# A product-key expert kernel: eight second-index rows in one operation, the gate moved into the first index's rows, and those rows dealt to three engines

## The chip, the cores and the metric

The kernel runs on one core of a Trainium2 chip. The metric is the device time of one execution in microseconds. Before the change three executions took 3919.23, 3922.02 and 3924.52 us; the median is 3922.02 us.

## The reference, cut to what matters

One inference step of a hybrid backbone, two layers over 128 context tokens and 512 latent tokens, all in float32. Each layer has a mixing half (pooling, gated linear attention, windowed attention) and a retrieval half; the change lies in the second:

```python
def _peer(h, wq, subkeys, u, v):
    q = (hf @ wq).reshape(n, PEER_HEADS, 2, PEER_QUERY_DIM // 2)
    s = jnp.einsum('nhpd,hpkd->nhpk', q, subkeys).astype(jnp.float32)
    sv, si = lax.top_k(s, PEER_TOPK)
    cand = (sv[:, :, 0, :, None] + sv[:, :, 1, None, :]).reshape(n, PEER_HEADS, PEER_TOPK * PEER_TOPK)
    cand_idx = (si[:, :, 0, :, None] * PEER_N_KEYS + si[:, :, 1, None, :]).reshape(n, PEER_HEADS, PEER_TOPK * PEER_TOPK)
    top_v, top_pos = lax.top_k(cand, PEER_TOPK)
    experts = jnp.take_along_axis(cand_idx, top_pos, axis=-1)
    gates = jax.nn.softmax(top_v, axis=-1).astype(h.dtype)
    ...
        act = jax.nn.gelu(jnp.einsum('td,tkd->tk', xb, u[eb]), approximate=False)
        return jnp.einsum('tk,tkd->td', gb * act, v[eb])
```

So each token picks 128 experts (8 heads, 16 each) out of 128 x 128, each given by a first index i, a second index j and a gate.

## The kernel before, in words

The 640 tokens are five blocks of 128. Blocks 0 and 1 gather the rows of their experts. The other three (`DB`, latent tokens) go the dense way: TensorE multiplies their activations with the whole table (`u_stage`, 128 stages of j), ScalarE applies Gelu, VectorE multiplies with a gate matrix G, and TensorE multiplies with the second table (`v_stage`). G is zero but for the 128 chosen experts of a token.

G is made in the stage that the change touches. For each of the three blocks (k = 1, 2, 3 in the code, blocks 1 to 3 in this text) TensorE turns the indices and gates so that the 128 choices of a token lie along the partitions (`turn`), and ScalarE copies them out (`turned_out`, L1706 to L1714) to `ijgT`: first index, second index, gate. Then each token gets two one-hot matrices of 128 choices by 128 keys: A marks the first index (`agrp`), B the second with the gate as its value (`bring`). TensorE multiplies them (`place`, L1907): one product is the 128 x 128 gate matrix of the token. In the trace each such product is two records, so a group of four tokens is 8 records.

A block is eight steps of 16 tokens; a step is four groups of four tokens, g0 to g3 below. Groups are numbered n over all blocks. Who makes what:

- B: VectorE, 16 operations of 128 columns in a step (`scatter_rows`, L1542), in a ring of 16 tokens.
- A: a ring of four groups (`A_GRP`). ScalarE marks the even n, g0 and g2 (`mark_rows`: four Abs of key minus index, then one Relu of 1 - x over all four tokens, L1726 and L1728). GpSimd marks the odd n, g1 and g3 (L1374).
- ScalarE also takes each group's product out of PSUM (`spread`, L1738), and after the evacuation of group n it marks group n + 4. There are two PSUM banks for the products:

```python
                        if n >= 2:
                            pe.wait_ge(g_out, n - 1)
```

so TensorE starts group n when group n - 2 has been evacuated.

No scheduler stands behind this: every engine's order is written by hand, and semaphores join them. `b_made`, `a_made` and `p_made` count finished one-hots, `g_mm` finished groups, `g_out` evacuated groups, `tr_out` turned indices. VectorE runs the routing of the next token block (top 16, candidates, indices, `route`) between the steps of `scatter_rows`; a new block's `turn` needs that routing's end (`gated`, after ScalarE's Exp in L1698). TensorE fills the time between steps with queries, scores and, in blocks 2 and 3, with `u_stage`. In block 1 ScalarE has other work in between: the square and the root of the fifth row block (L1656, L1661, L1662), copies of queries, turned rows and scores (L1680, L1670, L1674, L1690).

Of the kernel before, what the change touches and what calls it, by code (L numbers as in the profile page):

```python
# [12 lines left out]
ALU = mybir.AluOpType  # L13
# [27 lines left out]
JGRP = 4  # L41
CHUNK = 32
UR, VR, GR = 3, 3, 3
A_GRP, B_TOK = 4, 16
ADA_RING = 5
NMOD = 6 * KT

# [15 lines left out]
def build(nc, a, out, depth=DEPTH):  # L63
    sems = []

    def sem(name):
        s = nc.alloc_semaphore(name)
        sems.append(s)
        return s
# [102 lines left out]
    sc_mm, sc_ready, sc_read = sem("sc_mm"), sem("sc_ready"), sem("sc_read")  # L172
    ex_in, ex_out, ij_ready = sem("ex_in"), sem("ex_out"), sem("ij_ready")
    tr_mm, tr_out, a_made, b_made = sem("tr_mm"), sem("tr_out"), sem("a_made"), sem("b_made")
    p_made = sem("p_made")
    g_mm, g_out, g_sent = sem("g_mm"), sem("g_out"), [sem("g_sent0"), sem("g_sent1")]
    ut_mm, ut_gelu, ut_gated, vt_mm = sem("ut_mm"), sem("ut_gelu"), sem("ut_gated"), sem("vt_mm")
    routed, row_used = sem("routed"), sem("row_used")
# [184 lines left out]
    for l in range(depth):  # L363
# [913 lines left out]
        with nc.Block() as block:  # L1277
# [84 lines left out]
            @block.gpsimd  # L1362
            def _(pool):
                for n in range(ND // 4):
                    if act_marks(n):
                        continue
                    d, q = n // (P // 4), n % (P // 4)
                    if n < A_GRP:
                        pool.wait_ge(x_kept, 16 * len(DB))
                    pool.wait_ge(tr_out, d + 1)  # L1370
                    if n >= A_GRP:
                        pool.wait_ge(g_mm, n - A_GRP + 1)
                    for t in range(4):
                        pool.tensor_scalar(agrp[n % A_GRP][:, t], iota128[:, :], ijgT[:, d % 2, 0, 4 * q + t:4 * q + t + 1], 0.0,  # L1374
                                           ALU.add, ALU.is_equal).then_inc(p_made, 1)
                pool.wait_ge(sc_mm, NB)
                pool.wait_ge(routed, 1)
                for at in range(NROWS):
                    kind, b = ROUNDS[at // SLOTS]
                    q = at % SLOTS  # L1380
                    tab = tab_u if kind == "u" else tab_v
                    if at == EARLY - 2:
                        pool.wait_ge(g_mm, ND // 4)
                    if at == FIRST:
                        pool.wait_ge(routed, 2)
                    if before[at] is not None:
                        pool.wait_ge(row_used, before[at] + 1)
                    pool.indirect_dma_start(ring[slots[at]], None, tab, bass.IndirectOffsetOnAxis(  # L1388
                        ap=eidx[:, b * SLOTS + q:b * SLOTS + q + 1], axis=0)).then_inc(row_landed[slots[at]], 16)

            @block.vector
            def _(dve):
# [141 lines left out]
                def scatter_rows(d, step):  # L1534
                    if step == 0:
                        dve.wait_ge(tr_out, d + 1)
                        dve.wait_ge(x_kept, 16 * len(DB))
                    for t in range(16 * step, 16 * step + 16):
                        n = d * P + t
                        if n >= B_TOK and t % 4 == 0:  # L1540
                            dve.wait_ge(g_mm, (n - B_TOK) // 4 + 1)
                        dve.tensor_scalar(bring[:, n % B_TOK], iota128[:, :], ijgT[:, d % 2, 1, t:t + 1],  # L1542
                                          ijgT[:, d % 2, 2, t:t + 1], ALU.is_equal, ALU.mult).then_inc(b_made, 1)

                residual(0)
                mean(0)
# [103 lines left out]
            def _(act):  # L1650
# [55 lines left out]
                def turned_out(d):  # L1706
                    act.wait_ge(tr_mm, d + 1)
                    if d == 0:
                        act.wait_ge(xn_ready, 4)
                    if d >= 2:  # L1710
                        act.wait_ge(b_made, (d - 1) * P)
                        act.wait_ge(p_made, (d - 1) * (P // 2))
                    c.link(act.activation(ijgT[:, d % 2, 0], ps[:, 0, 0:P], ACT.Copy, scale=-1.0))
                    act.activation(ijgT[:, d % 2, 1:3].rearrange("p a t -> p (a t)"), ps[:, 0, P:3 * P], ACT.Copy).then_inc(tr_out, 1)  # L1714

                def mark_rows(n):
                    if not act_marks(n):
                        return
                    if n < A_GRP:
                        act.wait_ge(x_kept, 16 * len(DB))  # L1720
                    if n >= A_GRP:
                        act.wait_ge(g_mm, n - A_GRP + 1)
                    d, q = n // (P // 4), n % (P // 4)
                    four = agrp[n % A_GRP]
                    for t in range(4):
                        c.done(act.activation(four[:, t], iota128[:, :], ACT.Abs, bias=ijgT[:, d % 2, 0, 4 * q + t:4 * q + t + 1]))  # L1726
                    c.wait()
                    act.activation(four, four, ACT.Relu, scale=-1.0, bias=1.0).then_inc(a_made, 1)  # L1728

                def spread(d, step):  # L1730
                    for q in range(4 * step, 4 * step + 4):
# [80 lines left out]
            def _(pe):  # L1812
# [83 lines left out]
                def place(d, step):  # L1896
                    for q in range(4 * step, 4 * step + 4):
                        n = d * (P // 4) + q
                        if act_marks(n):
                            pe.wait_ge(a_made, n // 2 + 1)  # L1900
                        else:
                            pe.wait_ge(p_made, 4 * (n // 2) + 4)
                        pe.wait_ge(b_made, 4 * n + 4)
                        if n >= 2:
                            pe.wait_ge(g_out, n - 1)
                        for t in range(4):
# [197 lines left out]
```

## Time and profile before

| what | value |
|---|---|
| median of three runs | 3922.02 us |
| the profiled execution | 3926.03 us |
| its span, first to last instruction | 3924.2 us |
| TensorE busy | 3672.1 us (94%) |
| VectorE busy | 2581.9 us (66%) |
| ScalarE busy | 734.4 us (19%) |
| GpSimd busy | 1639.5 us (42%) |
| mean granted TensorE clock | 0.975 |

The profile is of one execution. The shares are means over the whole span; the stage of the change lies at 455 to 747 us in the first layer and about 1922 us later in the second. In rows, PE is TensorE, PEld its weight loads, DVE is VectorE, ACT ScalarE, POOL GpSimd; ps is PSUM, x and modbc hold the one-hots. "idle before" is how long an engine stood before an instruction, with the instruction that ended the wait as the profile infers it. A wait for several semaphores is put down to the one that the profile saw last. The granted clock is in tenths or shares of full speed.

### The profile page before, as it was taken

How to read it: one execution, taken by the hardware profiler on the slowest of the kernel's cores; microseconds unless marked ns; L12 is line 12 of the kernel's file. 1: busy time of each engine (PE TensorE's matmuls, PEld its weight loads, DVE VectorE, ACT ScalarE, POOL GpSimd, SP SyncE). 2: the span in 40 equal slices, each digit the busy share in tenths (PEclk: the TensorE clock that was granted, in tenths of full speed). 3: DMA queues.
4: the chain of work that ended last, by engine and by line, in shares of the span. 5: the costliest groups of instructions: out<-in, count | busy, mean ns of one | idle time of the engine just before them, and what ended most of it. 6: DMA issues, size and time to landing. Idle time of an engine off the chain costs nothing. (4 is left out here: it accounts for less than half of the span.)

```text
span 3924.2 us, 39919 instructions
## 1 busy us (share of the span) xinstructions
PE 3672.1 (94%) x13726; PEld 2101.5 (54%) x13726; DVE 2581.9 (66%) x5919; ACT 734.4 (19%) x1630; POOL 1639.5 (42%) x1498
## 2 busy tenths in 40 slices
PE   4888888999999999999989897889999999999997
PEld 3545676655555555554455566765555555555543
DVE  6783798767666666776624748878677546566444
ACT  1143465300000000000013525651000000000000
POOL 0210155356566644445402004544677655445340
PEclk9999999999999999999999998999999999999999
DMA  6323134689999999999830122447999999989774
GB/s 249 114 85 119 37 104 135 223 299 403 380 368 381 372 379 375 368 380 358 356 128 2 61 108 64 136 124 271 362 410 410 388 355 354 363 338 359 299 294 158
DMA packets 365385, 1026.96 MB, mean 262 GB/s; under 512 B 30848, under 2 KB 132480, under 8 KB 364416
## 3 DMA queue, kind: packets, MB, share of 16 engines
q0 software_dynamic: 147456, 536.94, 35.8%
q1 hardware_dynamic: 118352, 436.07, 29.0%
q10 hardware_dynamic: 99376, 51.40, 4.7%
q8 instruction: 111, 1.82, 0.2%
q14 instruction: 90, 0.74, 0.1%
HBM read 965.07 MB, written 59.22 MB: 261 GB/s over the span
## 5 line engine op out<-in xcount | busy, mean ns | idle before, releaser
L1881 PE MATMUL ps<-colsT,arena 128*128 128x384 f32 x4096 | 1359.0, 486 | 5.6 <-DMA arena<-in_peer_ut 5.6
L1881 PEld LDWEIGHTS ps<-colsT,arena 128*128 128x128 f32 x4096 | 775.8, 190 | 584.4 <-issue 94.7
L1916 PE MATMUL ps<-arena 128*128 128x512 f32 x1536 | 676.5, 592 | 0.0
L1388 POOL DMA_INDIRECT proj<-in_peer_u,eidx x336 | 473.0, 1408 | 247.1 <-DVE modbc L1582 121.5
L1388 POOL DMA_INDIRECT proj<-in_peer_v,eidx x335 | 360.7, 1077 | 313.7 <-DVE colsT L1593 213.9
L1916 PEld LDWEIGHTS ps<-arena 128*128 128x128 f32 x1536 | 291.8, 190 | 345.2 <-issue 317.6
L1374 POOL TENSOR_SCALAR x<-iota,modbc 128x128 f32<-128x128 f32 x192 | 145.5, 772 | 724.0 <-ACT modbc L1714 556.0
L1582 DVE CUSTOM_DVE_ANT_0 proj<-proj,rows 128x1024 f32<-128x1024 f32 x336 | 399.3, 1222 | 60.9 <-DMA proj<-in_peer_u,eidx 57.7
L1593 DVE SCALAR_TENSOR_TENSOR colsT<-proj,modbc,colsT 128x1024 f32<-128x1024 f32 x330 | 410.0, 1287 | 14.9 <-DMA proj<-in_peer_v,eidx 13.4
L1916 PE MATMUL ps<-arena,x 128*128 128x512 f32 x768 | 337.7, 592 | 0.0
L1916 PE MATMUL ps<-arena,rows 128*128 128x512 f32 x768 | 337.7, 592 | 0.0
L1388 POOL DMA_INDIRECT modbc<-in_peer_v,eidx x177 | 201.7, 1139 | 323.9 <-DVE colsT L1593 260.8
L1388 POOL DMA_INDIRECT modbc<-in_peer_u,eidx x176 | 228.6, 1299 | 223.2 <-DVE modbc L1582 181.0
L1704 ACT ACTIVATE arena<-ps 128x384 f32<-128x384 f32 x128 | 62.9, 491 | 1079.7 <-PE ps L1881 998.0
L232 DVE CUSTOM_DVE_ANT_0 proj<-proj,modbc 128x1024 f32<-128x1024 f32 x48 | 58.9, 1227 | 310.7 <-DMA proj<-in_w_adaT 303.1
L1542 DVE TENSOR_SCALAR x<-iota,modbc 128x128 f32<-128x128 f32 x768 | 215.3, 374 | 59.3 <-PE ps L1907 51.1
L1916 PEld LDWEIGHTS ps<-arena,rows 128*128 128x128 f32 x768 | 145.9, 190 | 173.4 <-issue 160.7
L1916 PEld LDWEIGHTS ps<-arena,x 128*128 128x128 f32 x768 | 145.9, 190 | 173.4 <-issue 160.7
L1582 DVE CUSTOM_DVE_ANT_0 modbc<-modbc,rows 128x1024 f32<-128x1024 f32 x176 | 211.6, 1222 | 32.8 <-DMA modbc<-in_peer_u,eidx 30.4
L1593 DVE SCALAR_TENSOR_TENSOR colsT<-modbc,colsT 128x1024 f32<-128x1024 f32 x174 | 220.3, 1293 | 8.0 <-DMA modbc<-in_peer_v,eidx 8.0
L574 PE MATMUL ps<-colsT,arena 128*128 128x512 f32 (+3 forms) x640 | 182.3, 446 | 16.6 <-PEq L143 10.7
L1374 POOL TENSOR_SCALAR modbc<-iota,modbc 128x128 f32<-128x128 f32 x192 | 162.7, 862 | 12.7 <-PE ps L1907 12.7
(304 smaller groups left out, 3722.1 us busy)
## 6 DMA issues: line engine op xcount, KB each, us to landing
arena<-in_peer_ut SPq DMA_DIRECT2D x256, 512.0 KB
arena<-in_peer_v SPq DMA_DIRECT2D x256, 512.0 KB
gmat_d<-arena ACTq DMA_DIRECT2D x24, 2048.0 KB, 9.3
arena<-gmat_d SPq DMA_DIRECT2D x64, 768.0 KB
proj<-in_w_adaT SPq DMA_DIRECT2D x51, 512.0 KB, 18.4
modbc<-in_w_adaT SPq DMA_DIRECT2D x19, 512.0 KB, 9.8
rows<-in_w_adaT SPq DMA_DIRECT2D x18, 512.0 KB, 3.6
arena<-in_w_in SPq DMA_DIRECT2D x2, 4224.0 KB, 16.5
```

The lines of the kernel that those rows point to most:

```text
L232: c.done(dve.tensor_tensor_reduce(out=junk, in0=tile, in1=silu_rows[0], scale=1.0, scalar=0.0, op0=ALU.mult, op1=ALU.add, accum_out=ada_co ...
L574: mm = pe.matmul(ps[0:w, banks(n)[seg], 0:m], wt[:, k, c0:c0 + w], hT[:, k, t0:t0 + m], start=(k == 0), stop=(k == KT - 1))
L1374: pool.tensor_scalar(agrp[n % A_GRP][:, t], iota128[:, :], ijgT[:, d % 2, 0, 4 * q + t:4 * q + t + 1], 0.0, ALU.add, ALU.is_equal).then_in ...
L1388: pool.indirect_dma_start(ring[slots[at]], None, tab, bass.IndirectOffsetOnAxis(ap=eidx[:, b * SLOTS + q:b * SLOTS + q + 1], axis=0)).then ...
L1542: dve.tensor_scalar(bring[:, n % B_TOK], iota128[:, :], ijgT[:, d % 2, 1, t:t + 1], ijgT[:, d % 2, 2, t:t + 1], ALU.is_equal, ALU.mult).th ...
L1582: dve.tensor_tensor_reduce(out=row, in0=row, in1=rb[:, b], scale=1.0, scalar=0.0, op0=ALU.mult, op1=ALU.add, accum_out=dots[:, b, q:q + 1] ...
L1593: dve.scalar_tensor_tensor(out=ysum[q % 2], in0=row, scalar=coef[:, b, q:q + 1], in1=ysum[q % 2], op0=ALU.mult, op1=ALU.add).then_inc(row_ ...
L1704: act.activation(wT[j % CR], ps[:, 2 + j % 2, 0:ND], ACT.Gelu).then_inc(ut_gelu, 1)
L1881: mm = pe.matmul(ps[:, 2 + j % 2, 0:ND], utab[:, j % UR, k], hT[:, k, NG:T], start=(k == 0), stop=(k == KT - 1))
L1916: mm = pe.matmul(ps[:, Y_BANKS[2 * d + c2], :], wT[j % CR][:, d * P:(d + 1) * P], vtab[:, j % VR, c2 * 512:(c2 + 1) * 512], start=(j == 0) ...
```

## The change

B loses its gate and is made eight tokens at a time, by comparing the keys with eight broadcast indices (`B_SET`). The gate moves into A. A's groups are dealt out anew: ScalarE keeps g0 and g2, GpSimd keeps g1, and VectorE makes g3, at the end of each of its steps, with two operations of 512 columns. ScalarE's Relu becomes gate - 2x, whose bias is a column for each token, so it is four operations of 128. `turned_out` is one copy of 384 columns, since the first index no longer changes sign.

```diff
@@ -41,7 +41,7 @@
 JGRP = 4
 CHUNK = 32
 UR, VR, GR = 3, 3, 3
-A_GRP, B_TOK = 4, 16
+A_GRP, B_TOK, B_SET = 4, 16, 8
 ADA_RING = 5
 NMOD = 6 * KT
 
@@ -172,7 +172,7 @@
     sc_mm, sc_ready, sc_read = sem("sc_mm"), sem("sc_ready"), sem("sc_read")
     ex_in, ex_out, ij_ready = sem("ex_in"), sem("ex_out"), sem("ij_ready")
     tr_mm, tr_out, a_made, b_made = sem("tr_mm"), sem("tr_out"), sem("a_made"), sem("b_made")
-    p_made = sem("p_made")
+    p_made, m_made = sem("p_made"), sem("m_made")
     g_mm, g_out, g_sent = sem("g_mm"), sem("g_out"), [sem("g_sent0"), sem("g_sent1")]
     ut_mm, ut_gelu, ut_gated, vt_mm = sem("ut_mm"), sem("ut_gelu"), sem("ut_gated"), sem("vt_mm")
     routed, row_used = sem("routed"), sem("row_used")
@@ -1362,7 +1362,7 @@
             @block.gpsimd
             def _(pool):
                 for n in range(ND // 4):
-                    if act_marks(n):
+                    if n % 4 != 1:
                         continue
                     d, q = n // (P // 4), n % (P // 4)
                     if n < A_GRP:
@@ -1371,8 +1371,9 @@
                     if n >= A_GRP:
                         pool.wait_ge(g_mm, n - A_GRP + 1)
                     for t in range(4):
-                        pool.tensor_scalar(agrp[n % A_GRP][:, t], iota128[:, :], ijgT[:, d % 2, 0, 4 * q + t:4 * q + t + 1], 0.0,
-                                           ALU.add, ALU.is_equal).then_inc(p_made, 1)
+                        tok = 4 * q + t
+                        pool.tensor_scalar(agrp[n % A_GRP][:, t], iota128[:, :], ijgT[:, d % 2, 0, tok:tok + 1],
+                                           ijgT[:, d % 2, 2, tok:tok + 1], ALU.is_equal, ALU.mult).then_inc(p_made, 1)
                 pool.wait_ge(sc_mm, NB)
                 pool.wait_ge(routed, 1)
                 for at in range(NROWS):
@@ -1535,12 +1536,23 @@
                     if step == 0:
                         dve.wait_ge(tr_out, d + 1)
                         dve.wait_ge(x_kept, 16 * len(DB))
-                    for t in range(16 * step, 16 * step + 16):
+                    for t in range(16 * step, 16 * step + 16, B_SET):
                         n = d * P + t
-                        if n >= B_TOK and t % 4 == 0:
-                            dve.wait_ge(g_mm, (n - B_TOK) // 4 + 1)
-                        dve.tensor_scalar(bring[:, n % B_TOK], iota128[:, :], ijgT[:, d % 2, 1, t:t + 1],
-                                          ijgT[:, d % 2, 2, t:t + 1], ALU.is_equal, ALU.mult).then_inc(b_made, 1)
+                        if n >= B_TOK:
+                            dve.wait_ge(g_mm, (n - B_TOK + B_SET) // 4)
+                        dve.tensor_tensor(bring[:, n % B_TOK:n % B_TOK + B_SET],
+                                          iota128[:, :].unsqueeze(1).to_broadcast([P, B_SET, NKEY]),
+                                          ijgT[:, d % 2, 1, t:t + B_SET].unsqueeze(2).to_broadcast([P, B_SET, NKEY]),
+                                          ALU.is_equal).then_inc(b_made, 1)
+                    n = d * (P // 4) + 4 * step + 3
+                    t = 16 * step + 12
+                    four = agrp[n % A_GRP]
+                    if n >= A_GRP:
+                        dve.wait_ge(g_mm, n - A_GRP + 1)
+                    c.link(dve.tensor_tensor(four, iota128[:, :].unsqueeze(1).to_broadcast([P, 4, NKEY]),
+                                             ijgT[:, d % 2, 0, t:t + 4].unsqueeze(2).to_broadcast([P, 4, NKEY]), ALU.is_equal))
+                    dve.tensor_tensor(four, four, ijgT[:, d % 2, 2, t:t + 4].unsqueeze(2).to_broadcast([P, 4, NKEY]),
+                                      ALU.mult).then_inc(m_made, 1)
 
                 residual(0)
                 mean(0)
@@ -1708,10 +1720,11 @@
                     if d == 0:
                         act.wait_ge(xn_ready, 4)
                     if d >= 2:
-                        act.wait_ge(b_made, (d - 1) * P)
-                        act.wait_ge(p_made, (d - 1) * (P // 2))
-                    c.link(act.activation(ijgT[:, d % 2, 0], ps[:, 0, 0:P], ACT.Copy, scale=-1.0))
-                    act.activation(ijgT[:, d % 2, 1:3].rearrange("p a t -> p (a t)"), ps[:, 0, P:3 * P], ACT.Copy).then_inc(tr_out, 1)
+                        act.wait_ge(b_made, (d - 1) * (P // B_SET))
+                        act.wait_ge(p_made, (d - 1) * (P // 4))
+                        act.wait_ge(m_made, (d - 1) * (P // 16))
+                    act.activation(ijgT[:, d % 2].rearrange("p a t -> p (a t)"), ps[:, 0, 0:3 * P], ACT.Copy).then_inc(tr_out, 1)
+                    act.wait_ge(tr_out, d + 1)
 
                 def mark_rows(n):
                     if not act_marks(n):
@@ -1723,9 +1736,13 @@
                     d, q = n // (P // 4), n % (P // 4)
                     four = agrp[n % A_GRP]
                     for t in range(4):
-                        c.done(act.activation(four[:, t], iota128[:, :], ACT.Abs, bias=ijgT[:, d % 2, 0, 4 * q + t:4 * q + t + 1]))
+                        tok = 4 * q + t
+                        c.done(act.activation(four[:, t], iota128[:, :], ACT.Abs, scale=-1.0, bias=ijgT[:, d % 2, 0, tok:tok + 1]))
                     c.wait()
-                    act.activation(four, four, ACT.Relu, scale=-1.0, bias=1.0).then_inc(a_made, 1)
+                    for t in range(4):
+                        tok = 4 * q + t
+                        act.activation(four[:, t], four[:, t], ACT.Relu, scale=-2.0,
+                                       bias=ijgT[:, d % 2, 2, tok:tok + 1]).then_inc(a_made, 1)
 
                 def spread(d, step):
                     for q in range(4 * step, 4 * step + 4):
@@ -1897,10 +1914,12 @@
                     for q in range(4 * step, 4 * step + 4):
                         n = d * (P // 4) + q
                         if act_marks(n):
-                            pe.wait_ge(a_made, n // 2 + 1)
+                            pe.wait_ge(a_made, 4 * (n // 2) + 4)
+                        elif n % 4 == 1:
+                            pe.wait_ge(p_made, 4 * (n // 4) + 4)
                         else:
-                            pe.wait_ge(p_made, 4 * (n // 2) + 4)
-                        pe.wait_ge(b_made, 4 * n + 4)
+                            pe.wait_ge(m_made, n // 4 + 1)
+                        pe.wait_ge(b_made, 4 * n // B_SET + 1)
                         if n >= 2:
                             pe.wait_ge(g_out, n - 1)
                         for t in range(4):
```

ScalarE at the start of a block, from the copy of the turned indices on (`turned_out`, the first `mark_rows`, `spread` of step 0; arena is where a product is evacuated to). Before:

```order
L1713 ACTIVATE modbc<-ps 128x128
L1714 ACTIVATE modbc<-ps 128x256
L1726 ACTIVATE x<-iota,modbc 128x128 x4
L1728 ACTIVATE x<-x 128x512
L1726 ACTIVATE modbc<-iota,modbc 128x128 x4
L1728 ACTIVATE modbc<-modbc 128x512
L1738 ACTIVATE arena<-ps 128x128x4
L1726 ACTIVATE x<-iota,modbc 128x128 x4
L1728 ACTIVATE x<-x 128x512
L1738 ACTIVATE arena<-ps 128x128x4 x2
```

Now:

```order
L1726 ACTIVATE modbc<-ps 128x384
L1740 ACTIVATE x<-iota,modbc 128x128 x4
L1744 ACTIVATE x<-x,modbc 128x128 x4
L1740 ACTIVATE modbc<-iota,modbc 128x128 x4
L1744 ACTIVATE modbc<-modbc 128x128 x4
L1755 ACTIVATE arena<-ps 128x128x4
L1740 ACTIVATE x<-iota,modbc 128x128 x4
L1744 ACTIVATE x<-x,modbc 128x128 x4
L1755 ACTIVATE arena<-ps 128x128x4 x2
```

Each mark has four instructions in the place of its one wide one; a mark still stands between the first evacuation and the next two.

VectorE at steps 6 and 7 of block 1 (one-hots, then pieces of routing; L1445 begins the search for the first index). Before:

```order
L1542 TENSOR_SCALAR x<-iota,modbc 128x128 x16
L1520 MAX proj<-proj 128x8 x8
L1523 MAX_INDEX proj<-proj 128x8 x8
L1525 CAST proj<-proj 128x128
L1542 TENSOR_SCALAR x<-iota,modbc 128x128 x16
L1445 TENSOR_TENSOR proj<-proj,ranks 128x2048
```

Now:

```order
L1543 TENSOR_TENSOR x<-iota,modbc 128x1024 x2
L1552 TENSOR_TENSOR modbc<-iota,modbc 128x512
L1554 TENSOR_TENSOR modbc<-modbc 128x512
L1521 MAX proj<-proj 128x8 x8
L1524 MAX_INDEX proj<-proj 128x8 x8
L1526 CAST proj<-proj 128x128
L1543 TENSOR_TENSOR x<-iota,modbc 128x1024 x2
L1552 TENSOR_TENSOR modbc<-iota,modbc 128x512
L1554 TENSOR_TENSOR modbc<-modbc 128x512
L1446 TENSOR_TENSOR proj<-proj,ranks 128x2048
```

Sixteen narrow operations became two wide ones and the two of g3, in front of the same routing.

## Rows read from the trace of the kernel before

**Rows 1.** Busy time by stretch (length, then each engine's busy us with instructions, granted clock, DMA):
```profile
455.00:557.00 102.00, 77.75 (x534) 72.51 (x532) 86.85 (x363) 59.24 (x136) 51.08 (x64) 0.90 0.32 93
557.00:650.00 93.00, 81.00 (x465) 63.12 (x464) 78.97 (x346) 55.05 (x127) 51.47 (x64) 0.96 0.48 146
650.00:747.00 97.00, 86.39 (x420) 63.51 (x421) 76.75 (x345) 53.87 (x127) 51.41 (x64) 0.95 0.43 127
747.00:2380.00 1633.00, 1586.97 (x5449) 850.02 (x5447) 1041.43 (x1902) 195.25 (x418) 676.52 (x555) 0.99 0.76 291
```

**Rows 2.** Timeline, step 2 of block 3 (start, length, engine, line, operation, [idle before, releaser]):
```profile
678.09 1.13 PE L1907 MATMUL ps<-x,modbc 128*128 128x128 f32 x8
680.40 1.13 PE L1907 MATMUL ps<-x,modbc 128*128 128x128 f32 x8 [1.18 <-ACT arena L1738]
...
677.84 1.27 ACT L1726 ACTIVATE x<-iota,modbc 128x128 f32<-128x128 f32 x4
679.14 0.63 ACT L1728 ACTIVATE x<-x 128x512 f32<-128x512 f32 x1
679.68 1.07 ACT L1738 ACTIVATE arena<-ps 128x512 f32<-128x512 f32 x2
...
678.38 3.07 POOL L1374 TENSOR_SCALAR x<-iota,modbc 128x128 f32<-128x128 f32 x4 [3.73 <-PE ps L1907]
```

**Rows 3.** Groups by shape, whole run (busy us, mean ns, idle before, releasers):
```profile
L1907 PEld LDWEIGHTS ps<-x,modbc 128*128 128x128 f32 x768 | 100.0, 204 | 49.7 <-POOL x L1374 45.3 <-issue 2.2
```

**Rows 4.** Timeline, start of block 2, ScalarE and TensorE:
```profile
557.11 0.28 ACT L1713 ACTIVATE modbc<-ps 128x128 f32<-128x128 f32 x1 [1.58 <-PE ps L1893]
557.70 1.26 ACT L1726 ACTIVATE x<-iota,modbc 128x128 f32<-128x128 f32 x4
558.99 0.63 ACT L1728 ACTIVATE x<-x 128x512 f32<-128x512 f32 x1
559.53 1.26 ACT L1726 ACTIVATE modbc<-iota,modbc 128x128 f32<-128x128 f32 x4
...
559.72 3.75 PE L1907 MATMUL ps<-x 128*128 128x128 f32 x16 [2.65 <-DVE x L1542]
563.27 2.72 PE L1907 MATMUL ps<-x,modbc 128*128 128x128 f32 x16
```

**Rows 5.** Timeline, start of block 1, ScalarE and VectorE:
```profile
465.91 0.60 ACT L1738 ACTIVATE arena<-ps 128x512 f32<-128x512 f32 x1 [1.28 <-PE ps L1907]
472.07 1.05 ACT L1656 ACTIVATE rows<-x 128x1024 f32<-128x1024 f32 x1
479.77 0.60 ACT L1738 ACTIVATE arena<-ps 128x512 f32<-128x512 f32 x1 [0.20 <-PE ps L1907]
...
486.25 0.16 DVE L1420 TENSOR_TENSOR stats<-stats 128x1 f32<-128x1 f32 x1 [4.51 <-ACT stats L1662]
```

**Rows 6.** Timeline, steps 4 and 5 of block 1, ScalarE:
```profile
513.35 0.60 ACT L1738 ACTIVATE arena<-ps 128x512 f32<-128x512 f32 x1 [0.17 <-ACT modbc L1690]
...
519.81 1.08 ACT L1674 ACTIVATE colsT<-ps 128x512 f32<-128x512 f32 x2 [0.76 <-PE ps L1834]
```

**Rows 7.** Timeline, end of block 1, VectorE and GpSimd:
```profile
537.22 1.17 DVE L1542 TENSOR_SCALAR x<-iota,modbc 128x128 f32<-128x128 f32 x4 [0.66 <-PE ps L1907]
538.31 2.37 DVE L1445 TENSOR_TENSOR proj<-proj,ranks 128x2048 f32<-128x2048 f32 x1
540.71 2.34 DVE L1447 TENSOR_TENSOR proj<-proj 128x2048 f32<-128x2048 f32 x1
...
553.98 0.29 DVE L1469 TENSOR_TENSOR proj<-proj 128x128 f32<-128x128 f32 x1
...
537.35 6.29 POOL L1374 TENSOR_SCALAR modbc<-iota,modbc 128x128 f32<-128x128 f32 x4 [0.18 <-PE ps L1907]
```

**Rows 8.** Groups by shape, whole run, a two-input operation of 1024:
```profile
L1407 DVE TENSOR_TENSOR x<-x,rows 128x1024 f32<-128x1024 f32 x10 | 12.3, 1228 | 0.3
```

**Rows 9.** Timeline, end of block 2, VectorE:
```profile
649.91 0.28 DVE L1474 TENSOR_REDUCE proj<-proj 128x8 f32<-128x128 f32 x1 [6.45 <-ACT proj L1698]
```

## The prediction

> **What bounds the kernel now.** I read the busy time by stretch first, then the order of time on TensorE, then on the engines that it waits for. [rows 1] has the stage that the change touches, in the first layer: its three blocks of 128 latent tokens take 102, 93 and 97 us (the second layer repeats them), and the long stretch behind them has TensorE busy for 1587 of 1633 us. So what the stage loses on TensorE is not won back later. Inside the stage no engine is full over all three blocks: TensorE is busy 78, 81 and 86 us, VectorE 87, 79 and 77, ScalarE 54 to 59, GpSimd 51. The answer is in the waits.
>
> In each step of 16 tokens TensorE does four groups g0 to g3. From step 2 of block 1 on, g0 to g2 run without a gap and then TensorE stands 1.18 us before g3 [rows 2]. The same 1.18 us stands in 16 steps of a layer (steps 3, 4, 5 and 6 of block 1, and 1 to 6 of blocks 2 and 3); step 2 of block 1 has nearly as much. What ends it is in ScalarE's order. Behind the evacuation of g0 it marks a coming group (four Abs in 1.27 us, one wide Relu), and only then comes the evacuation of g1, which frees the PSUM bank that g3 needs. Two evacuations take 1.07 us from 679.68, so the first ends near 680.26; TensorE resumes at 680.40. The table of groups says otherwise: it gives 45.3 us of the weight loads' idle time to GpSimd [rows 3]. I don't follow it. GpSimd works at 678.38 to 681.45 [rows 2] on a group of the next step, and the wait ends in the middle of that.
>
> **The edit on ScalarE.** A mark is now four Abs and four narrow Relus. The wide Relu costs 679.68 - 679.14 = 0.54 us to the next start. Four narrow instructions with a bias column take 1.27 us from first start to last end [rows 2], and the next instruction starts about 0.09 before an end (679.14 + 0.63 against 679.68): 1.18 us. So a mark grows by 1.18 - 0.54, about 0.63 us. No row shows a Relu with a bias column; the Abs is the nearest, with the same shape and operand. As bounds: the 128-wide copy takes 0.28 us [rows 4], overlapped some 0.19, four of them 0.75: a mark grows by 0.2. With no overlap at all, four of (1.27 + 3 x 0.09) / 4 = 0.39 are 1.56: it grows by 1.0.
> The Trainium skill ("ScalarE: Activation LUTs", What ACT_TABLE_LOAD costs) speaks against this edit: 186 ns plus 0.833 ns an element, 93 ns more for each pointer operand, 93 ns of overlap. By that the four cost 1.18 us and the wide one 0.52, a mark grows by 0.66, and the sum below would be 35 us in place of 34. No row here has the new instruction to check it with.
>
> **Where that stands on TensorE's path.** Per layer:
> - Blocks 2 and 3, steps 1 to 6: one mark lies between the evacuations of g0 and g1, so the 1.18 becomes 1.81. 6 x 0.63 = 3.8 us in each. The second mark of a step is hidden under the expert matmuls or queries that follow g3 [rows 2].
> - Start of block 2 [rows 4]: ScalarE copies the turned indices (two instructions now, one of 384 columns after: 557.11 to 557.70 becomes some 0.07 shorter), then makes two marks, then evacuates. TensorE's first matmul, 559.72, follows the end of the first mark at 559.62, not VectorE's first four tokens. With marks of 2.46 us (1.83 before, 557.70 to 559.53, and 0.63) and 0.49 from one evacuation's start to the next: 557.63 + 2 x 2.46 + 0.49 + 2.46 + 0.60 = 566.1 us for the end of g1's evacuation. g3 began at 564.86 (the run of g2 and g3 ends at 563.27 + 2.72, and a group takes 1.13). The granted clock is at half speed there, which hides part. Loss 1.3 us. Block 3 starts alike; its g3 ran at the low clock and would run at the full one, so 1.0 us.
> - Block 1, step 0: four marks stand before the square of the fifth row block, but TensorE at half clock paces most of it. The first evacuation stays near 465.95 (VectorE's first tokens come 0.1 later, and ScalarE's first two marks end at 465.7). From there ScalarE has an evacuation, a mark, two evacuations, a mark, an evacuation: 0.49 + 2.46 + 0.49 + 0.49 + 2.46 + 0.49 = 6.88, so the square starts at 472.83 against 472.07 [rows 5]. 0.8 us, and VectorE waits for that square.
> - Block 1, step 1: two marks before the root that VectorE waits for at 486.25 [rows 5]: 1.26, less 0.2 of idle that they fill, 1.0 us. Step 2: one mark, 0.6.
> - Block 1, steps 3 to 6: here ScalarE itself is full. After step 3's last evacuation it copies rows and scores until 513.35 and TensorE waits for it [rows 6]. Two marks of step 3, one of step 4 (the second falls into the 0.76 us before 519.81), one of step 5, one of step 6: 5 x 0.63 = 3.2.
> - End of block 1 [rows 7]: VectorE waits at 537.22 for g3 of step 6, makes the last four tokens (1.09 us to 538.31), and then runs 16 us of routing (to 554.27) that TensorE's next block waits for. After the change eight tokens and the new fourth group stand behind that same wait. A wide TENSOR_TENSOR of 1024 takes 1.23 [rows 8], one of 2048 2.34 [rows 7]; that makes 512 cost about 0.69. To the next start: 1.15 + 0.73 (linked) + 0.61 = 2.5 us against 1.1. Loss 1.4 us. Block 2 has the same growth at its end, but VectorE stands 6.45 us there for ScalarE's Exp [rows 9], which waits for TensorE: hidden.
> Layer: 3.8 + 3.8 + 1.3 + 1.0 + 0.8 + 1.0 + 0.6 + 3.2 + 1.4 = 16.9 us. Two layers: **34 us**.
>
> **The edits that I cost at nothing.** VectorE: sixteen tokens cost 16 x 0.27 = 4.3 us, and now 1.15 + 1.15 + 0.73 + 0.61 = 3.6: 0.5 to 0.7 less in each of 48 steps, 25 to 34 us of VectorE's time. But from step 3 on the order on TensorE never waits for these tokens; VectorE is ahead by most of a step and stands for TensorE itself. The cover is that lead; if it were gone, 3.6 us of a step would still come sooner than before. The first eight tokens arrive about 0.1 us later than the first four did, at the first two steps alone, inside the sums above. GpSimd: half its marks go. It keeps g1, which it makes a step ahead, so its time buys nothing. Its marks may stretch: beside VectorE's 2048-wide operations four of them take 6.29 us in place of 3.1 [rows 7]. Even 6.3 us is under the 10 us of a step. The fourth group moves to VectorE behind the tokens, 3.6 us after a step's start there; TensorE comes to it last.
>
> **The sum.** The profiled execution took 3926.03 us (span 3924.2), 4 us over the median of 3922.02. 3926.0 + 33.8 = 3959.8 for a profiled one; against the median, 3922.0 + 33.8 = **3956 us**. With the low bound of the mark (0.2) the starts cost nothing and the rest 1.2 + 1.2 + 1.4 + 1.4 = 5.2 a layer: 3932. With the high one (1.0) it is 28 a layer: 3978.
>
> **The rivals.**
> *A, the waits are GpSimd's (faster).* As [rows 3] has it, TensorE waits before g3 for GpSimd's marks. Then giving g3 to VectorE removes up to 45 us: 3877. It decides where GpSimd's mark of g3 ends later than the evacuation of g1. For it: the table, and GpSimd's four marks in 6.29 us beside wide operations [rows 7]. Against: the times in [rows 2]. Chance 0.06.
> *B, VectorE sets the pace (faster).* In block 1 it is busy 87 of 102 us. If all 48 steps were its own, 25 us go: 3897. Against: 1.18 us waits that VectorE's rows don't end, and its own idle time in blocks 2 and 3. Chance 0.04.
> *C, hidden.* The longer marks fit beside TensorE's work, or what VectorE saves in block 1 pays for them: within 8 us of 3922. Against: the 1.18 us exist already, so nothing is left to hide under. Chance 0.05.
> *D, VectorE blocked by GpSimd (slower still).* Four wide two-input operations a step now meet GpSimd's four marks of some 0.79 us each. If each had to wait one out, a step costs VectorE 3.2 us more; in block 1, where it is nearly full, 8 x 3.2 - 4 = 21 us a layer in place of the 7 of my sum: 3984. Against: L1445 and L1447 took 2.37 and 2.34 us beside GpSimd's marks; GpSimd stood, and VectorE lost under 0.1 [rows 7]. Chance 0.05.
> The Trainium skill ("SBUF — State Buffer", Who interferes with whom) has the rule behind D: a VectorE instruction with two SBUF inputs and a GpSimd instruction that reads SBUF exclude each other, and the one issued first blocks the other. By that rule D could come about; the trace agrees for GpSimd (6.29 us for four), not for VectorE (under 0.1 us).
>
> **How the numbers follow.** The forecast has 0.80. A difference under 0.2% (8 us) can't be told from none. Faster: A and B, 0.10. Same: C, 0.05. Slower: forecast and D, 0.85. The range 3932 to 3978 is the forecast with the two bounds of a mark; A, B, C and D, 0.20, lie outside.
>
> **What would show it.** In the changed profile: the gap before g3 1.8 us in 16 steps a layer; four Relus near 1.2 us; g3's start in block 2 later by 1.3; TENSOR_TENSOR of 1024 at 1.2 us, GpSimd's marks longer yet ended well before g1. Blocks 1 to 3 should take 109, 98 and 102 us. The forecast is wrong if the gap before g3 stays or goes (A), if TensorE begins to wait for VectorE's tokens (D), or if narrow Relus start less than 0.2 us apart. Further drops of the granted clock in block 1, where TensorE stands longest, would add to it.

## The result, and the profile after

| | before | changed |
|---|---|---|
| median | 3923.27 us (3919.23 to 3925.28, 4 runs) | 3983.57 us (3978.79 to 3985.28, 4 runs) |
| profiled execution | 3926.03 us | 3984.22 us |
| its span | 3924.2 us | 3982.4 us |
| ratio | | 1.0152, 95% interval 1.014 to 1.0163 |

The change makes the kernel 60 us slower. The forecast said slower, by 34 us, with a range that ended at 3978: the direction was right, the size was not.

Busy time by stretch, the counterpart of [rows 1] with each stretch cut at TensorE's turns of the indices. First the whole stage of each layer (length, then busy us and instructions of PE, PEld, DVE, ACT, POOL, then granted clock and DMA) in the kernel before:

```profile
454.73:741.79 287.06, 240.19 (x1402) 196.34 (x1403) 237.49 (x1048) 167.83 (x388) 153.96 (x192) 0.93 0.40 120
2376.45:2663.49 287.04, 240.21 (x1402) 196.35 (x1403) 237.54 (x1048) 167.81 (x388) 153.80 (x192) 0.93 0.40 120
```

and the same in the changed kernel, with the three blocks of the first layer behind:

```profile
454.68:766.51 311.83, 246.44 (x1402) 200.34 (x1403) 218.12 (x757) 198.41 (x529) 101.50 (x96) 0.92 0.37 110
2403.39:2719.76 316.37, 253.82 (x1402) 207.33 (x1403) 218.36 (x757) 198.55 (x529) 101.34 (x96) 0.89 0.37 109
...
454.68:565.45 110.77, 79.31 (x532) 73.28 (x532) 81.70 (x267) 69.63 (x183) 30.08 (x32) 0.89 0.30 86
565.45:670.15 104.70, 86.17 (x467) 67.14 (x467) 73.05 (x252) 65.28 (x174) 35.08 (x32) 0.92 0.43 131
670.15:766.51 96.36, 80.96 (x404) 59.93 (x405) 63.37 (x238) 63.51 (x172) 36.34 (x32) 0.95 0.39 115
```

The two stages took 574.1 us and take 628.2: 54 of the 58 us by which the spans differ. These lines split the 54. TensorE runs the same matmuls in each stage (1402 records). Its idle time (length minus busy) was 93.7 us in both stages together and is 127.9: **34 us more standing**. Its busy time for the same matmuls was 480.4 and is 500.3: **20 us more for the same work**, while the granted clock fell from 0.93 to 0.92 and 0.89. VectorE is 39 us less busy in the two stages, GpSimd 105 us less, and ScalarE 61 us more. The other 4 us of the 58 lie outside the stages, where TensorE is busy as long as before (3191.7 and 3192.5 us); what makes them was not looked into.

Block by block, with both kernels' stretches taken from turn to turn, TensorE's busy time grew by 1.8 and 5.6 us in block 1 of the two layers, by 4.7 and 6.0 in block 2 and by -0.2 and 2.0 in block 3: most of the slow work came in block 2.

The steady step, as in [rows 2] (timeline, step 5 of block 2, TensorE, ScalarE, GpSimd):

```profile
629.07 1.13 PE L1926 MATMUL ps<-x,modbc 128*128 128x128 f32 x8
632.02 1.13 PE L1926 MATMUL ps<-x,modbc 128*128 128x128 f32 x8 [1.82 <-ACT arena L1755]
...
628.83 1.26 ACT L1740 ACTIVATE x<-iota,modbc 128x128 f32<-128x128 f32 x4
630.12 1.27 ACT L1744 ACTIVATE x<-x,modbc 128x128 f32<-128x128 f32 x4
631.30 1.05 ACT L1755 ACTIVATE arena<-ps 128x512 f32<-128x512 f32 x2
...
629.36 4.14 POOL L1375 TENSOR_SCALAR x<-iota,modbc 128x128 f32<-128x128 f32 x4 [7.02 <-PE ps L1926]
```

The mark between the two evacuations lasts from 628.83 to 631.30, 2.47 us against 1.84 before, and the gap before g3 went from 1.18 to 1.82 us. It stands in 17 steps of the first layer and 16 of the second. GpSimd works on past 632.02 here too, so it did not end the wait.

The start of block 2, as in [rows 4]:

```profile
565.45 0.33 PE L1908 MATMUL ps<-ident,proj 128*128 128x128 f32 x1 [2.21 <-DVEq L1480]
569.24 2.04 PE L1926 MATMUL ps<-x 128*128 128x128 f32 x8 [3.25 <-ACT x L1744]
572.51 2.08 PE L1926 MATMUL ps<-x 128*128 128x128 f32 x8 [1.22 <-POOL x L1375]
574.38 3.62 PE L1926 MATMUL ps<-x,modbc 128*128 128x128 f32 x16
...
566.55 2.36 DVE L1543 TENSOR_TENSOR x<-iota,modbc 128x1024 f32<-128x1024 f32 x2 [1.22 <-ACT modbc L1726]
566.62 5.83 POOL L1375 TENSOR_SCALAR x<-iota,modbc 128x128 f32<-128x128 f32 x4 [20.54 <-ACT modbc L1726]
```

Here is something that [rows 4] did not have: TensorE waits 1.22 us for GpSimd before g1. Four of GpSimd's operations take 5.83 us beside VectorE's wide ones. This stands at the start of all six blocks (1.21 or 1.22 us). TensorE's wait before g0 has grown too, to 3.25 us from 2.65, since ScalarE's first mark is longer.

The end of block 1, as in [rows 7]:

```profile
545.76 1.23 DVE L1543 TENSOR_TENSOR x<-iota,modbc 128x1024 f32<-128x1024 f32 x1 [2.67 <-PE ps L1926]
546.90 0.69 DVE L1552 TENSOR_TENSOR modbc<-iota,modbc 128x512 f32<-128x512 f32 x1
547.62 0.69 DVE L1554 TENSOR_TENSOR modbc<-modbc 128x512 f32<-128x512 f32 x1
548.24 2.28 DVE L1446 TENSOR_TENSOR proj<-proj,ranks 128x2048 f32<-128x2048 f32 x1
```

548.24 - 545.76 = 2.48 us between the end of the wait and the routing, where 1.09 stood before.

What the forecast lacks is the clock's part. A run of two gaps in the second layer shows it (timeline, step 3 of block 2, and the stretch of time behind it):

```profile
2557.90 2.02 PE L1926 MATMUL ps<-x,modbc 128*128 128x128 f32 x8 [1.82 <-ACT arena L1755]
...
2546.00:2557.90 11.90, 9.09 (x48) 6.79 (x49) 8.95 (x28) 9.68 (x26) 4.10 (x5) 1.00 0.53 157
2557.90:2561.40 3.50, 3.50 (x11) 2.83 (x12) 1.44 (x2) 3.26 (x10) 1.48 (x2) 0.51 0.00 0
```

The group behind the gap takes 2.02 us in place of 1.13: at 0.51 TensorE is granted 1.2 of its 2.4 GHz. Not every gap does this: behind the 33 gaps of 1.82 us in the two layers, 8 groups took 1.59 us or more in place of 1.13. Behind the 32 gaps of 1.18 us in the kernel before it was 2. There, block 2 of the first layer, which began at 556.52, was granted the full clock from 8 us after its start on:

```profile
564.70:649.80 85.10, 75.95 (x443) 58.11 (x441) 72.01 (x316) 47.86 (x109) 44.66 (x55) 1.00 0.53 158
```

### The profile page after: what moved, and what is told of

Read it like the earlier page. It is cut to its first block and busy times, and to the rows that moved or that the text cites. A ratio compares the mean times of both kernels' runs of the same rounds, so it can differ in the third digit from the quotient of the medians.

```text
span 3982.4 us, 39393 instructions
## 1 busy us (share of the span) xinstructions
PE 3692.8 (93%) x13726; PEld 2116.2 (53%) x13726; DVE 2546.3 (64%) x5343; ACT 795.1 (20%) x1912; POOL 1531.7 (38%) x1306
## 3 DMA queue, kind: packets, MB, share of 16 engines
q8 instruction: 111, 1.82, 0.2%
## 5 line engine op out<-in xcount | busy, mean ns | idle before, releaser
L1375 POOL TENSOR_SCALAR x<-iota,modbc 128x128 f32<-128x128 f32 x192 | 202.8, 1067 | 882.6 <-ACT modbc L1726 583.1
L1543 DVE TENSOR_TENSOR x<-iota,modbc 128x1024 f32<-128x1024 f32 x96 | 116.5, 1226 | 143.3 <-PE ps L1926 137.4
L1926 PE MATMUL ps<-x,modbc 128*128 128x128 f32 x768 | 121.9, 313 | 64.6 <-ACT arena L1755 64.6
```

The lines of the kernel that those rows point to most:

```text
L1543: dve.tensor_tensor(bring[:, n % B_TOK:n % B_TOK + B_SET], iota128[:, :].unsqueeze(1).to_broadcast([P, B_SET, NKEY]), ijgT[:, d % 2, 1, t: ...
L1926: mm = pe.matmul(ps[:, n % 2, t * P:(t + 1) * P], agrp[n % A_GRP][:, t], bring[:, (4 * n + t) % B_TOK], start=True, stop=True)
```

## The experiments

Medians in us. "Idle" and "busy" are TensorE's in the two stages together, from the same view as above: the length of the stage less busy, and busy. The kernel before: 93.7 and 480.4. Each ratio is to the kernel before, run beside that group of experiments: its medians were 3923.3 for the changed kernel, 3924.2 for e1 to e4, 3926.7 for e5 to e8 and 3922.8 for e9 and e10. A comparison across the groups is safer by the ratios.

| run | median | ratio to before (95%) | idle | busy |
|---|---|---|---|---|
| changed kernel | 3983.6 | 1.0152 (1.014 to 1.0163) | 127.9 | 500.3 |
| e1 narrow Relus alone | 3967.5 | 1.0111 (1.0094 to 1.0128) | 127.1 | 486.0 |
| e2 changed, wide Relu | 3939.1 | 1.0037 (1.0022 to 1.0051) | 103.7 | 486.9 |
| e3 before, evacuations first | 3889.7 | 0.991 (0.9893 to 0.9926) | 65.5 | 474.3 |
| e4 changed, evacuations first | 3928.5 | 1.0016 (1.0007 to 1.0026) | 94.8 | 484.8 |
| e5 changed, gaps filled | 3967.5 | 1.0102 (1.0085 to 1.0119) | 84.7 | (with the fill) 532.3 |
| e6 changed, narrow start | 3976.9 | 1.0123 (1.0104 to 1.0141) | 130.6 | 494.2 |
| e7 before, wide B | 3933.3 | 1.0015 (1.0006 to 1.0025) | 99.5 | 481.8 |
| e8 changed, GpSimd makes g3 | 3978.3 | 1.0131 (1.0113 to 1.0148) | 126.6 | 499.8 |
| e9 e3 and fill behind the turn | 3890.4 | 0.9924 (0.9907 to 0.994) | 58.6 | (with the fill) 478.3 |
| e10 e3 and fill on both sides | 3889.5 | 0.9921 (0.9904 to 0.9938) | 52.3 | (with the fill) 484.0 |

### e1: the narrow Relus alone

```diff
-                    act.activation(four, four, ACT.Relu, scale=-1.0, bias=1.0).then_inc(a_made, 1)
+                    for t in range(4):
+                        act.activation(four[:, t], four[:, t], ACT.Relu, scale=-1.0, bias=ones[:, t:t + 1]).then_inc(a_made, 1)
```

> The kernel before with one edit: ScalarE's wide Relu becomes four narrow ones with a bias column, the gate stays in B. Theory: this edit on TensorE's path is most of the loss, and the added idle time lets the granted clock fall more often. Gap before g3 1.8 us, 16 times a layer, 14 us a layer for the marks at full clock, and half-clock time in the stage above the 75 us of before: 3950 to 3975 us. Rival (the other edits cost it: wide VectorE operations and GpSimd blocked by them): 3923 to 3930.

Measured 3967.5: 43 us of the 60, inside the theory's range. A step of block 3 (timeline, TensorE and ScalarE):

```profile
693.24 1.13 PE L1908 MATMUL ps<-x,modbc 128*128 128x128 f32 x8
696.19 1.13 PE L1908 MATMUL ps<-x,modbc 128*128 128x128 f32 x8 [1.82 <-ACT arena L1739]
...
692.99 1.27 ACT L1726 ACTIVATE x<-iota,modbc 128x128 f32<-128x128 f32 x4
694.29 1.28 ACT L1729 ACTIVATE x<-x,ones 128x128 f32<-128x128 f32 x4
695.47 1.06 ACT L1739 ACTIVATE arena<-ps 128x512 f32<-128x512 f32 x2
```

The gap is 1.82 with this edit alone, so the mark makes it. TensorE's idle time grew by 33.4 us and its busy time by 5.6; behind its 32 gaps of 1.82 us, 6 groups took 1.75 us or more in place of 1.13. The trace's clock records give the half clock 82 us of the two stages, against 75 before. The forecast's sum for this edit (without the 1.4 us a layer of VectorE's) was 31.

### e2: the changed kernel with the wide Relu

The reverse edit, in the changed kernel. It leaves the gate out of the rows that ScalarE makes.

> The changed kernel with the wide Relu of before in ScalarE's marks (the gate is left out of g0 and g2). Theory: gap before g3 back at 1.18 us; what stays is GpSimd's blocked first mark of a block and VectorE's longer end of block 1, 2 to 4 us a block: 3930 to 3945 us. Rival (VectorE and GpSimd cost it): still above 3965.

Measured 3939.1, inside the theory's range and far under the rival's. The step's gap is back (timeline, block 2):

```profile
606.03 1.13 PE L1923 MATMUL ps<-x,modbc 128*128 128x128 f32 x8
608.34 1.13 PE L1923 MATMUL ps<-x,modbc 128*128 128x128 f32 x8 [1.18 <-ACT arena L1752]
```

All the other edits together cost 15 us: 10 us of idle time and 6.5 of longer busy time. e1 and e2 add up to 58 of the 60 us.

### e3 and e4: ScalarE's evacuations ahead of its mark

```diff
-                        if q + A_GRP < P // 4:
-                            mark_rows(n + A_GRP)
+                        if q % 2 == 1 and q - 1 + A_GRP < P // 4:
+                            mark_rows(n - 1 + A_GRP)
```

> The kernel before, ScalarE's order alone changed: the evacuation of g1 comes before the mark, so no mark stands between the evacuations of g0 and g1. Theory: the 1.18 us before g3 goes in most of 32 steps, 25 to 38 us, perhaps more through the clock: 3875 to 3900. Rival A (the wait is for GpSimd's marks): the gap stays and the time is that of before, 3923.

> The changed kernel with the same order of ScalarE. Theory: the 1.82 us before g3 goes (up to 58 us) and with it the extra half-clock time (up to 20 us): 3905 to 3930. Rival A: no change, 3984. If the clock does not follow the gaps: about 3928 and as much half-clock time as in the changed kernel.

Measured 3889.7 and 3928.5, that is 34 us less and 55 less. e3 came out as its theory had it. e4 is inside its range too, but the time alone doesn't decide there: "about 3928" was also the figure for a clock that does not follow the gaps. The rows decide. TensorE's standing fell by 33.1 us, not by 58, its busy time by 15.5, and the half clock had 102 us of the stages in place of 119 (75 in the kernel before, by the traces' clock records), so the clock did follow, if not all the way. A step of block 3 in e3 (timeline, TensorE and ScalarE):

```profile
656.56 1.95 PE L1907 MATMUL ps<-x 128*128 128x128 f32 x16
658.40 2.02 PE L1907 MATMUL ps<-x,modbc 128*128 128x128 f32 x16
660.26 5.33 PE L1881 MATMUL ps<-colsT,arena 128*128 128x384 f32 x16
...
657.65 0.60 ACT L1738 ACTIVATE arena<-ps 128x512 f32<-128x512 f32 x1 [0.40 <-PE ps L1907]
658.55 0.60 ACT L1738 ACTIVATE arena<-ps 128x512 f32<-128x512 f32 x1 [0.29 <-PE ps L1907]
659.04 1.26 ACT L1726 ACTIVATE x<-iota,modbc 128x128 f32<-128x128 f32 x4
```

g0 to g3 run as one, with nothing changed for GpSimd. The row of [rows 3] in e3 (groups by shape, whole run):

```profile
L1907 PEld LDWEIGHTS ps<-x,modbc 128*128 128x128 f32 x768 | 98.9, 208 | 12.5 <-issue 8.8 <-ACT modbc L1728 1.5 <-POOL modbc L1374 0.9
```

That settles rival A: of the 45.3 us that [rows 3] puts down to GpSimd, ScalarE's order alone leaves 0.9. With this order the changed kernel is 4 us slower than the kernel before without it; the pair e3 and e4 still differ by 39 us, 29 of them standing. In e4 the gap before g3 is gone from the long steps, but other waits are longer. In block 1, TensorE waits for an evacuation that stands behind a long mark and ScalarE's copies (timeline of e4, block 1):

```profile
520.67 3.65 PE L1926 MATMUL ps<-x,modbc 128*128 128x128 f32 x16 [3.60 <-ACT arena L1755]
...
529.03 2.02 PE L1926 MATMUL ps<-x,modbc 128*128 128x128 f32 x16 [2.04 <-ACT arena L1755]
```

In e3 the same two waits are 2.78 and 1.02 us. In blocks 2 and 3 of e4 TensorE waits 1.22 us for GpSimd at each start, as in the changed kernel, and again later (1.07 us in block 2, 1.89 in block 3).

e3 beats both kernels: 0.991 of the time before.

### e5: the gaps filled

```diff
+                        if d >= 1 and 1 <= step < G_STEPS - 1 and q % 4 == 3:
...
+                            for _ in range(8):
+                                pe.matmul(ps[:, 2 + j % 2, 0:P], ident[:, :], ident[:, :], start=True, stop=True)
```

> The changed kernel, with eight 128x128 matmuls of the identity (about 1.8 us, result unused) put in TensorE's order before g3 in steps 1 to 6 of blocks 2 and 3. The gap keeps its length and TensorE is busy in it. If the granted clock falls because of the gaps: half-clock time in blocks 2 and 3 from 61 us to about 35, and 12 us off the time, 3968 to 3976. If the clock does not follow the gaps: as the changed kernel, 3984, or above it where the fill is longer than the gap.

Measured 3967.5, a little under the range for a clock that follows the gaps, and 16 us under the changed kernel (19 by the ratios), with intervals that don't meet. The gap has its length still, now full (timeline, TensorE, block 2):

```profile
608.19 1.13 PE L1933 MATMUL ps<-x,modbc 128*128 128x128 f32 x8
609.15 1.95 PE L1929 MATMUL ps<-ident 128*128 128x128 f32 x16
611.05 1.16 PE L1933 MATMUL ps<-x,modbc 128*128 128x128 f32 x8
```

TensorE did more work in the same program and finished sooner. By the clock records the half clock had 34 us of blocks 2 and 3 before (both layers), 61 in the changed kernel and 44 here, where 35 were expected. These four blocks are 10.9 us shorter. Nothing but TensorE's order was changed, so most of the extra half clock of blocks 2 and 3 (17 of 27 us) comes from TensorE standing before g3; the rest this experiment leaves open.

### e6, e7, e8: what the other edits cost

e6 makes the second-index rows of step 0 of each block with narrow one-input operations:

```diff
+                        if step == 0:
+                            for u in range(t, t + B_SET):
+                                ins = dve.tensor_scalar(bring[:, (d * P + u) % B_TOK], iota128[:, :], ijgT[:, d % 2, 1, u:u + 1],
+                                                        ones[:, 0:1], ALU.is_equal, ALU.mult)
```

> The changed kernel, with the 16 second-index rows of step 0 of each block made by 16 narrow one-input operations in place of 2 wide two-input ones. Theory: GpSimd's first mark of a block is held up by the wide operations (5.8 us for four in place of about 3), and TensorE waits 1.2 us for g1 at the half clock; without them GpSimd needs 3.2 us, the wait goes and the blocks are 1.5 to 2.5 us shorter: 3970 to 3976. Rival (the starts are not it): 3984.

Measured 3976.9, 7 us under the changed kernel (11 by the ratios) and just over the range; the intervals of the two touch, so the size is loose. Its TensorE stood as long as before the edit (130.6 against 127.9) and was busy 6 us less. The wait before g1 went, but in its place TensorE now waits before g3 of the same step for ScalarE's evacuation behind a long mark, 0.55 to 1.67 us over the six blocks (timeline, TensorE, start of block 2):

```profile
576.23 1.18 PE L1932 MATMUL ps<-x,modbc 128*128 128x128 f32 x8
578.64 1.13 PE L1932 MATMUL ps<-x,modbc 128*128 128x128 f32 x8 [1.24 <-ACT arena L1761]
```

So at a block's start GpSimd and ScalarE's marks both hold TensorE up, and in part one hides the other. Step 0 of block 2 still ends 10.9 us after the turn in place of 12.5. In block 1 the narrow rows are ready later: its first group starts 1.0 us later behind the turn (10.16 us against 9.13). That GpSimd's stretch comes from VectorE's wide operations is plain in the timeline of GpSimd at the start of block 2, now 3.34 us where 5.83 stood:

```profile
570.05 3.34 POOL L1375 TENSOR_SCALAR x<-iota,modbc 128x128 f32<-128x128 f32 x4 [20.54 <-ACT modbc L1732]
```

e7 is the wide B alone in the kernel before (`dve.tensor_tensor` over eight tokens, the gate left out):

> The kernel before with the wide B alone (eight rows in one operation, the gate left out), marks and their engines as before. Theory: VectorE's shorter time buys nothing and GpSimd's held-up first marks cost 1 to 2 us a block: 3928 to 3938. Rival (VectorE sets the pace): below 3915.

Measured 3933.3, 0.15% slower: 6 us, with an interval of 2 to 10. VectorE's shorter time bought nothing, and the start of block 2 shows the new wait without any of the other edits (timeline):

```profile
563.36 2.07 PE L1909 MATMUL ps<-x 128*128 128x128 f32 x8 [1.05 <-POOL x L1374]
...
558.43 4.88 POOL L1374 TENSOR_SCALAR x<-iota,modbc 128x128 f32<-128x128 f32 x4 [12.82 <-ACT modbc L1716]
```

e8 gives g3 back to GpSimd and takes it from VectorE (the two wide operations of `scatter_rows` go, GpSimd marks every odd group):

> The changed kernel, but GpSimd makes g3 as well as g1 (with the gate), VectorE makes only B. Theory: the end of block 1 is 1.4 us a layer shorter; at a block's start GpSimd's second mark may come too late for g3, 0 to 3 us a block: 3978 to 3995. Rival A (TensorE waits for GpSimd's marks before g3 in every step): above 4010.

Measured 3978.3, just inside the expected range and 5 us under the changed kernel (8 by the ratios), with intervals that overlap: who makes g3 matters little, if at all. At the end of block 1 the routing starts 1.14 us after the wait in place of 2.48.

### e9 and e10: fill at the starts of blocks, on top of e3

```diff
+                        for _ in range(12):
+                            pe.matmul(ps[:, 1, 0:P], ident[:, :], ident[:, :], start=True, stop=True)
                     pe.wait_ge(tr_out, d + 1)
```

> The kernel before with the evacuations first (as e3), and 12 matmuls of the identity (about 2.7 us, result unused) behind the turn of the indices at the start of blocks 2 and 3, where TensorE stands 2.65 us. If the clock follows what TensorE did before: part of the 6.8 us of half clock at each of these four starts goes, 3 to 10 us in all against e3: 3880 to 3887. If not: as e3, 3890, or up to 4 us above.

> As e9, and 8 more matmuls of the identity ahead of the turn, where TensorE waits 1.8 and 3.1 us for the routing. If the clock follows what TensorE did before: nearly no half clock at the starts of blocks 2 and 3, 3874 to 3884. If the clock does not follow: as e3, 3890.

Both missed: 3890.4 and 3889.5, and the ratios to the kernel before, 0.9924 and 0.9921, are no lower than the 0.991 of e3. The clock did as expected: of the 6.8 us of half clock at each start of blocks 2 and 3, none is left in e10 and 3.4 us in one of four starts in e9. The time did not follow, because the start is not paced by TensorE alone (timeline of e10, start of block 2):

```profile
555.20 1.13 PE L1912 MATMUL ps<-x 128*128 128x128 f32 x8
556.51 1.16 PE L1912 MATMUL ps<-x 128*128 128x128 f32 x8 [0.19 <-POOL x L1374]
...
559.43 1.16 PE L1912 MATMUL ps<-x,modbc 128*128 128x128 f32 x8 [0.75 <-POOL modbc L1374]
```

At the full clock TensorE runs into GpSimd's marks, 0.19 us before g1 and 0.75 before g3. The granted clock over the start of block 2, and over the whole of it, in e3:

```profile
555.58:565.40 9.82, 7.17 (x36) 6.95 (x37) 8.47 (x36) 7.65 (x21) 8.45 (x12) 0.65 0.02 6
555.58:642.58 87.00, 80.61 (x467) 63.35 (x468) 79.89 (x348) 55.65 (x127) 48.47 (x64) 0.96 0.53 158
```

and in e10:

```profile
551.99:560.60 8.61, 7.67 (x60) 7.11 (x61) 7.29 (x32) 7.60 (x20) 7.24 (x10) 1.00 0.02 6
551.99:637.81 85.82, 82.93 (x508) 65.47 (x508) 80.05 (x348) 55.60 (x127) 46.05 (x64) 1.00 0.54 161
```

Block 2 is 1.2 us shorter, and blocks 2 and 3 of both layers together 3.2 us, in e9 as in e10: too little for these medians to show.

## Why the prediction was right in direction and wrong in size

- **What bounds the stage.** Right. ScalarE's mark between two evacuations ends TensorE's wait before g3; e3 removes it by order alone.
- **The price of a mark.** Right: 2.47 us against the forecast's 2.46, the gap 1.82 against 1.81. The page of the Trainium skill on ScalarE ("ScalarE: Activation LUTs", What ACT_TABLE_LOAD costs) gave 0.66 for the growth of a mark (0.65 when its figures are added up again); the runs show 0.63.
- **The standing time.** 33.8 us in the sum, 34.2 in the profile. In the sum it was all marks but for the 2.8 us at the ends of block 1; in the runs the marks alone give 33.4 (e1). The end of block 1 was right at 2.5 us. That the totals agree is in part luck. Blocks 2 and 3 stand 5.7 us longer each, where the sum had 5.1 and 4.8: the sum left out GpSimd's wait at the start and had there 1.3 and 1.0 for ScalarE's marks, where 1.8 stands (0.60 before g0, 1.22 before g1). Block 1 stands 7.2 us longer in the first layer and 4.4 in the second, where the sum had 7.0.
- **The edits that I cost at nothing: GpSimd.** Wrong. The step was "It keeps g1, which it makes a step ahead, so its time buys nothing", and that its stretched marks fit into the 10 us of a step. At a block's start there is no step ahead: the indices arrive, and g1 is due 1.8 us after g0. 5.83 us for four marks is late by 1.22. I had the stretch in [rows 7] and did not walk GpSimd through the start as I did ScalarE. All edits but the Relus cost 15 us (e2), the wide B alone some 6, with an interval of 2 to 10 (e7). How much of the changed kernel's loss is GpSimd's alone isn't separate from the marks, since e6 removed its wait and ScalarE's came in its place.
- **The clock.** Wrong, and this is what carried the result out of the range. The sum priced every stand of TensorE at its own length and put further drops of the clock at nothing: neither the 34 us nor the range, which had only the bounds of a mark, holds a term for them, and the last sentence of the prediction only said that they would add to it. They added 20 us: the same matmuls took 500.3 us in place of 480.4. Without these 20 us the result would be near 3964, inside the range. They also came elsewhere than the prediction looked for them: most in block 2, not in block 1.
- **The remaining 8 us.** The forecast and the 20 us of clock make 3976. Of the rest, 4 us lie outside the stages and aren't explained; the others are how the medians differ from the profiled executions and from the earlier median before.
- **VectorE and GpSimd, rival D.** VectorE's wide operations take 1.23 and 0.69 us beside GpSimd's marks, as priced; it was GpSimd that stood. The Trainium skill's rule that the one issued first blocks the other ("SBUF — State Buffer", Who interferes with whom) shows here for GpSimd alone: the 96 wide operations of 1024 never took more than 1.32 us, and that of 545.76 took 1.23 although GpSimd had been at its four marks since 541.94 (for 4.14 us). The 3984 that D had for the time is the measured time by coincidence.
- **Rivals A, B and C** fell: A with e3, B with e7, C with the result.

What stays open is why the clock's part varies. The narrow Relus alone make the same 1.82 us gaps and cost 5.6 us of busy time; the rest alone costs 6.5; together they cost 20. The half clock had 75 us of the two stages before, 82 in e1, 99 in e2 and 119 in the changed kernel, so it isn't the sum of its parts either. In e5 block 1 was granted 0.85 in the first layer and 0.89 in the second, with the same instructions (busy time by stretch):

```profile
457.55:568.94 111.39, 82.30 (x531) 76.82 (x532) 82.06 (x267) 69.95 (x183) 30.85 (x32) 0.85 0.30 86
2402.12:2512.90 110.78, 79.33 (x532) 73.28 (x532) 81.70 (x267) 69.62 (x183) 30.08 (x32) 0.89 0.30 86
```

So the 20 us are shown to be clock, and e5 shows that standing brings most of it in blocks 2 and 3, but how much a given gap brings was not found.

## What to carry to other kernels

An engine with 20% busy time can set the pace: ask what stands in its order between two things that another engine waits for, and put the release first. Swapping two calls on ScalarE gave 34 us. And when an edit lengthens a stall of TensorE, price the clock as well as the stall, with a range: here 33 to 34 us of standing brought 6 us more of slow matmuls in e1 and 20 in the changed kernel.

## What the runs showed of the hardware

- Matmuls whose result nobody uses, put into a 1.82 us wait of TensorE, at 24 places, made the kernel 16 us faster (e5). At the starts of blocks 2 and 3 they removed the half clock altogether (e10) and gained nothing that the medians show.
- Four 128-wide marks of GpSimd take 3.34 us beside VectorE's one-input operations, and 5.83 us beside its two-input ones of 1024 (e6 and the changed kernel, start of block 2); the latter keep their 1.23 us.
- Two losses were not the sum of their parts: marks and the rest cost 33.4 and 10.0 us of standing apart, 34.2 together. A part of the overlap is at a block's start, where e6 shows one wait taking the other's place: step 0 of block 2 ends 9.5 us after the turn in the kernel before, 10.9 in e1, 11.9 in e2 and 12.5 in the changed kernel, 3.1 us late where the two apart make 3.9. Where the rest lies was not looked into.
